# One range clear at each stage's end, and four heads written out, in a two-layer decoder step

## The reference

```
xn = rms_norm(x, norm_mix);  z = xn @ w_in          # all heads of all mixers, and 4 gates
A: retention                 S_t = gamma S_{t-1} + k_t^T v_t
B: HGRN2                     S_t = diag(f_t) S_{t-1} + k_t^T v_t
C: gated DeltaNet            S_t = g_t (I - beta_t k_t k_t^T) S_{t-1} + beta_t k_t v_t^T
D: differential attention    p0 - lam * p1, paged K/V cache for the sample tokens
h = x + (sum_b sigmoid(G_b xn) * (o_b @ W_b)) @ W_o
y = h + PEER(rms_norm(h))    # 8 x top-16 of 16384 single-neuron experts
```

## Time and profile before

| | us |
|---|---|
| three runs | 7348.95, 7351.94, 7352.01 |
| median | 7351.94 |
| the profiled execution, its own time | 7354.07 |
| its span in the trace | 7352.4 |
| TensorE busy | 6491.3 (88%) |
| VectorE busy | 3593.1 (49%) |
| ScalarE busy | 2128.9 (29%) |
| mean granted clock of TensorE | 0.92 |

### The profile page before, as it was taken

One profiled execution on the slowest core, in us unless ns is written; L12 is line 12 of the kernel. 1 busy time (PEld: TensorE's weight loads), 2 busy tenths in 40 slices (PEclk: granted clock), 3 DMA queues, 4 the chain that ended last, 5 costly groups with the idle time before them and its releaser, 6 DMA issues. The chain is left out here.

```text
span 7352.4 us, 111812 instructions
## 1 busy us (share of the span) xinstructions
PE 6491.3 (88%) x42878; PEld 6040.7 (82%) x42878; DVE 3593.1 (49%) x6555; ACT 2128.9 (29%) x3108; POOL 0.7 (0%) x6
## 2 busy tenths in 40 slices
PE   7787877797999997999977878777979999979999
PEld 5666666697999997999966666667979999979999
DVE  2332423333778885555423324233337788845554
ACT  2222222322224442222222222223222244422222
POOL 0000000000000000000000000000000000000000
PEclk8888878898999998999988878878989999989999
DMA  2111111222445665444321212102224456654443
GB/s 89 44 52 39 51 49 24 71 81 89 120 114 150 186 186 192 172 176 176 133 76 46 52 38 53 51 19 71 81 92 118 116 148 189 182 195 177 175 173 130
DMA packets 512751, 804.49 MB, mean 109 GB/s; under 512 B 83616, under 2 KB 321184, under 8 KB 494240
## 3 DMA queue, kind: packets, MB, share of 16 engines
q1 hardware_dynamic: 512464, 800.68, 34.6%
HBM read 616.20 MB, written 186.72 MB: 109 GB/s over the span
## 5 line engine op out<-in xcount | busy, mean ns | idle before, releaser
L1462 PE MATMUL ps<-xh,wh 128*128 128x288 f32 x4608 | 1376.3, 299 | 46.5 <-DVE wl L1678 46.5
L1462 PE MATMUL ps<-xl,wh 128*128 128x288 f32 x4608 | 1361.8, 296 | 0.0
L1462 PE MATMUL ps<-xh,wl 128*128 128x288 f32 x4608 | 1357.1, 295 | 0.0
L1878 PE MATMUL ps<-gh,vh 128*128 128x320 f32 (+1 forms) x4096 | 893.9, 300 | 77.7 <-DVE vl L1943 77.7
L160 PE MATMUL ps<-xn,wr 128*128 128x288 f32 x3072 | 843.5, 434 | 74.3 <-PEq L101 49.2
L1462 PEld LDWEIGHTS ps<-xh,wh 128*128 128x128 f32 x4608 | 867.1, 188 | 49.7 <-DVE wl L1678 47.4
L1878 PE MATMUL ps<-gl,vh 128*128 128x320 f32 (+1 forms) x4096 | 883.6, 297 | 0.0
L1878 PE MATMUL ps<-gh,vl 128*128 128x320 f32 (+1 forms) x4096 | 882.9, 297 | 0.0
L1462 PEld LDWEIGHTS ps<-xh,wl 128*128 128x128 f32 x4608 | 868.3, 188 | 0.0
L1462 PEld LDWEIGHTS ps<-xl,wh 128*128 128x128 f32 x4608 | 867.1, 188 | 0.0
L160 PEld LDWEIGHTS ps<-xn,wr 128*128 128x128 f32 x3072 | 619.3, 205 | 278.0 <-issue 76.9
(11 more groups left out here) (350 smaller groups left out, 8890.4 us busy)
## 6 DMA issues: line engine op xcount, KB each, us to landing
raw<-in_u SPq DMA_DIRECT2D x256, 512.0 KB, 4.2
vr<-in_v SPq DMA_DIRECT2D x512, 256.0 KB, 2.6
activated<-go SPq DMA_DIRECT2D x256, 288.0 KB, 4.5
coefficients<-wt SPq DMA_DIRECT2D x36, 2048.0 KB, 9.3
gb<-activated SPq DMA_DIRECT2D x64, 1152.0 KB, 5.9
wb<-coefficients SPq DMA_DIRECT2D x64, 1152.0 KB, 8.4
wr<-in_w_cm SPq DMA_DIRECT2D x104, 512.0 KB, 4.2
wm<-in_w_merge SPq DMA_DIRECT2D x32, 768.0 KB, 4.3
```

Of the source, the lines that this page charges most:

```text
L1462: last = nc.tensor.matmul(out, wp[:, slot, k, :], xp[:, k, cols], start=(k == 0 and wp is T.wh and xp is T.xh), stop=(k == KD - 1 and wp i ...
L1878: last = nc.tensor.matmul(out, vp[:, x % 4, m * P:(m + 1) * P], gp[:, row, col:col + size], start=begins, stop=False, skip_group_check=True)
```

## The change

The semaphores of a stage are cleared by their numbers instead of their names: the numbers are sorted, and for each unbroken run of them SP issues one `sem_clear` over the range. The loop over the first three heads is replaced by a loop of the building program over all four, so h is a constant everywhere and `more` is false for the last. The loop over the layers stays.

```diff
@@ stage
         with nc.Block(no_gpsimd_drain=True) as block:
             yield block, sems
-        for n in names:
-            nc.sync.sem_clear(sems[n])
+        numbers = sorted(sems[n].num for n in names)
+        for i in numbers:
+            if i - 1 not in numbers:
+                nc.sync.sem_clear(range(i, next(j for j in range(i, i + 256) if j not in numbers)))
         nc.all_engine_barrier(sem_only=True)
@@ program
                     norm_stage(nc, T, l, True)
                     first_head_stage(nc, T, l)
-                    with nc.Fori(0, H - 1) as h:
-                        head(nc, T, l, h, True)
-                    head(nc, T, l, H - 1, False)
+                    for h in range(H):
+                        head(nc, T, l, h, h < H - 1)
```

## The result

| | us |
|---|---|
| changed kernel, four runs | 7250.26 to 7258.29, median 7252.66 |
| kernel before, four runs | 7348.95 to 7352.02, median 7351.98 |
| ratio, 95% interval | 0.9867 (0.985 to 0.9884) |
| profiled execution | 7252.22, span 7250.6 |

The forecast was 7240 us and the range 7212 to 7280. The profiled executions differ by 101.9 us, where the sum had 111.8.

What follows compares the result with a forecast made beforehand. TensorE, busy 6491.3 of 7352.4 us, sets the time; its idle time can be won. 7354.1 - 76.7 - 14.4 - 0.7 - 20 = 7242.3 us, from an execution 2.1 us above the median, so 7240 us; range 7212 to 7280.

Steps and rivals of the forecast that it cites:

- The clears, 76.7 us: At every stage end, one clear per unbroken run of numbers: 1397 serial steps of 54.9 ns go, 76.7 us.
- The numbers are given out together: Assumption that a stage's semaphore numbers form one run when it opens, leaving 47 clears in all.
- rival C: At stage ends, a range clear costs by its numbers, or the numbers lie scattered: 7337 us, chance 0.08.
- The loop, 14.4 us: Ahead of a head's first product, four taken branches go, 3.44 to 3.77 us of TensorE idle time each.
- Straight code costs nothing: In the written-out heads, no stall from straight code; constant slots even gain 0.7 us over six heads.
- The clock, 20 us: Ahead of gdn and attention, shorter gaps avoid half of the clock falls: 20 us of a possible 40.
- in eight heads: Ahead of attention, a clock fall costing 2.1 us was taken to happen in eight heads.
- other falls that drop out: Clock falls elsewhere that vanish; with SP's hiccups, given only 8 us at the range's lower end.
- A: Ahead of gdn and attention, the clock never falls in the shortened gaps: 20 us more gain, 7220 us, chance 0.15.
- B: The clock gives nothing, as falls happen as often or move to other sparse stretches: 7260 us, chance 0.18.
- D: In heads 0 to 2, straight code starves TensorE, two stops a stage of 3.6 us: 7413 us, chance 0.05.

Runs made afterwards that it cites:

- The heads alone: Against the kernel before, only the loop over heads written out, each semaphore still cleared by itself: 7338.0 us, ratio 0.9979.

## Why the prediction was right, point by point

- **The clears, 76.7 us.** Right. The mechanism (serial at every stage end, 54.9 ns a step) holds: the gap ahead of gdn went from 3.81 to 2.25 us where 2.27 was forecast. Mis-sized by some 4 us: with the clears alone changed the path from clear to product is 72.9 us shorter (232.6 to 159.7). The reasons are 101 clears, and 1.7 ns a number in them. "The numbers are given out together" was the wrong assumption; a few extra runs cost little, as rival C said.
- **The loop, 14.4 us.** Right: 3.6 to 4.1 us a branch with the clears gone, where the forecast had 3.4 to 3.8; the step from the clears alone to the changed kernel shortens the path by 16.1 us (159.7 to 143.6). The heads alone gave 16.0 us.
- **Straight code costs nothing.** Nearly: no gap of TensorE with "issue" in the heads, but SP's queue pauses oftener in its rows of clears. With ranges there is no such row left to pause in.
- **The clock, 20 us.** It measured 12.9 us, and its working is wrong. The forecast had about half of the 16 shortened gaps keep the clock up, and none did in the changed kernel; gdn's first 32 products take 9.69 us, neither the 8.0 nor the 11 that it had named. Nor are there 16: "in eight heads" is wrong for attention, since head 3 starts it with other work, after 9.88 us of idle time before and 6.17 now. 4 x 3.5 us came from a fall in the middle of hgrn that went away, about 1.5 us a gdn stage in heads 1 and 2, most of it from a fall that lasts less long, and some was lost again in head 3 and in head 0. I had set this aside as "other falls that drop out"; it carries the term. That a positive term of this size came out is luck: code that changes nothing else moved the same balance by 10 us.
- **Rivals.** A came true only when the gaps got below 1.9 us. B, with falls that move to other stretches, describes what the clock did better than the forecast does, and its 7260 us is nearer to the 7252.7 measured than 7240 is. C's price by the number is real and thirty times smaller than its upper end. D did not show on TensorE.

## What to carry to other kernels

Look at what is serial at a stage's end before looking at busy time: 25 ns of busy hid 55 ns a step, 1397 times. Clear semaphores by range, and clear them while the next stage runs with other numbers; with the clear and its barrier off the path this kernel gained 15.6 us by their own length, and 21 more that are put down to TensorE's clock. When a change of 10 us in 7300 is to be judged on one core, vary something harmless: one clear and one barrier at the start moved this kernel by 10 us.

## What the runs showed of the hardware

- A range clear takes 25 ns for one number, 64 for 24, 132 for 63.
- At the starts of gdn and attention TensorE's clock went to 1.2 GHz after 2.2 to 2.5 us without products in 83 of 84 cases, after 1.86 to 1.89 us in 5 of 51. At the starts of hgrn it did so after 2.36 us in 5 of 14 and after 2.7 to 2.9 us in 8 of 10, and around a gap of 2.65 us in its middle in 55 of 104. A fall cost 1.7 us of dense products (9.69 against 8.00) in the changed kernel.
- Six products of 128 columns in the gap did not keep the clock up at 12 of 14 starts.
- A delay of 1.7 us at the start was gone by head 3: head 0's hgrn and gdn stages had become 3.2 us shorter.
